# Sampled attention with high and low queries side by side, stacked new values, and GpSimd at work: one change to a decoder-step kernel

## The chip, the cores and the metric

The kernel runs on one core of one Trainium2 chip. The metric is the device time of one execution in microseconds (us). TensorE (PE in the profile) multiplies matrices, VectorE (DVE) and ScalarE (ACT) do elementwise work, GpSimd (POOL) is a further engine that here may touch SBUF only, and SyncE (SP) issues DMAs.

## The reference

One layer of a hybrid decoder, for a prompt of 1024 tokens and for 8 sampled sequences of 8 new tokens each. The change lies in the attention of the sampled sequences, whose 1024 past keys and values lie in 8 pages of 128 rows:

```python
def sample_attn(q, k, v, lam, k_past, v_past, rel_bias):
    ...
    s_past = diff_logits(q, q_pos, k_past, jnp.arange(past, dtype=jnp.int32), rel_bias)
    s_new = diff_logits(q, q_pos, k, q_pos, rel_bias)
    w = diff_weights(jnp.concatenate([s_past, s_new], axis=-1), lam).astype(v.dtype)
    return (jnp.einsum('bhqk,bkhe->bqhe', w[..., :past], v_past)
            + jnp.einsum('bhqk,bkhe->bqhe', w[..., past:], v))
```

`diff_logits` is scaled q.k plus a bias by distance, masked; `diff_weights` is softmax of map 0 minus `lam` times softmax of map 1. There are 8 heads, each with 2 maps of 64 dimensions, so a sequence has 8 heads x 2 maps x 8 tokens = 128 rows of scores over 1032 keys. After it come a norm per head, gates, the output projection, and a channel mixer.

## The kernel before

Every fp32 product is made of reduced-precision (fp32r) ones: an operand is split by ScalarE into a rounded high part (`*_hi`, an `ACT.Copy`) and by VectorE into the rest (`*_lo`, a subtraction), and TensorE adds up hi.hi + hi.lo + lo.hi. The program has four stages: `front` and `heads` (the prompt, up to about 840 us), `sampled_and_out` (the sampled sequences, to about 1105 us, and the output projection), and `mixer`. The change is in `sampled_and_out`.

**Turns and slots.** `all_turns` calls each engine's `body(b, u)` for turns b = 0 to 8. In turn b the scores of sequence b are made (`has(b, 0)`), and the values of sequence b - 1 are multiplied (`has(b, 1)`). A turn runs over slots h: 0 to 8 on TensorE, 0 to 7 on the others. Each engine's queue is in program order, and they meet through counting semaphores. TensorE's slot h does, in order:

- `turn_keys(b, u, h)`: 8 transposes of the raw key pages of head h into two PSUM banks `tb[0]`, `tb[1]`, four each. Each half waits until `kt_lo` of the same half of the head before is made (`ktlo_done`), as it overwrites what that was read from. In slot 8 it is head 0 of the next sequence.
- in slot 0, `page(b - 1, 7)`: the last page of values of the sequence before.
- scores of head h - 1 into the three banks `S3` (344 keys each), which sum over all eight heads: the queries of a head stand in 16 columns of its own of a 128-column block that is otherwise zero, so that each head adds to its own 16 rows. Head 0 waits for `ttr_done`, since VectorE has to have read S3 of the sequence before.
- slot 2: `fold_heads`, 8 products that bring together the two halves of the rows of `o2s` (ScalarE's copy of the attention output `o2`).
- slot 3: `pt`, the weights transposed and signed by a product of P with C; its results are split into `pt_both` in slot 4.
- slots 4 and on: `page(b, n)` for the n of `PV_AT[h]`, 4 products of 512 columns each, which wait until `v_lo` of that page is made. The 8 new rows are a ninth page of 8 rows.

ScalarE's slot h: `keys(b, h)` (two copies to `kt_hi`, each after its half of the transposes, and a small one for the new keys), then in slot 1 the exponent and `copy_o2`, and then the high parts `v_hi` of the pages in `SPLIT_AT[h]`. VectorE's slot h: `keys` (two subtractions to `kt_lo`, and a small one), then `v_lo` of the same pages. At the end of a turn VectorE adds the bias to S3 with a running maximum (`tensor_tensor_reduce`, L2011), negates the maximum, and writes low queries. In turn 7 (`LAST`) both split parts of the output projection too, in the slots of `OUT_AT`, ahead of the pages of the same slot: `("m", 0)` is the first tile of merged activations, loaded by `load_m(0)`. In turn 8 the pages follow `SPLIT_LAST`.

SyncE issues all loads in program order too. In its turn b come the key pages of sequence b + 1 (after `tk_done`, at 16 b), in turns 7 and 8 instead four row blocks of w_out each (`ow_raw`), and in turn 7 then `load_m(0)` and `load_m(1)`; then value page 7 of sequence b - 1, and value pages 0 to 6 of sequence b, each after `page_done` of the same page of the sequence before, since `v_lo`, and with it `v_raw`, is read until then. `load_v(6, ...)` of the turn before, whose last wait is for page 6, stands ahead of `ow_raw` and `load_m(0)`.

GpSimd fills two query tiles with zeros at the stage's start and does nothing else in it.

## Time and profile before

| | us |
|---|---|
| median of 3 runs (lowest, highest) | 2076.24 (2076.22, 2077.07) |
| the profiled execution, its own time | 2075.18 |
| its span in the profile | 2073.4 |
| TensorE busy in the span | 2028.7 (98%) |
| VectorE, ScalarE, GpSimd busy | 1386.3 (67%), 993.4 (48%), 12.4 (1%) |

The spans below are of the one profiled execution, and count from the start of its span. The execution's own time is 1.8 us longer than its span. Busy shares are means over the whole program; what sets the time of a stage is to be read within it. A matmul's listed duration runs over into the next one's; what it costs in a row of matmuls is the distance between two starts.

### The profile page before, as it was taken

How to read it: one execution, taken by the hardware profiler on the slowest of the kernel's cores; microseconds unless marked ns; L12 is line 12 of the kernel's file. 1: busy time of each engine (PE TensorE's matmuls, PEld its weight loads, DVE VectorE, ACT ScalarE, POOL GpSimd, SP SyncE). 2: the span in 40 equal slices, each digit the busy share in tenths (PEclk: the TensorE clock that was granted, in tenths of full speed). 3: DMA queues.
4: the chain of work that ended last, by engine and by line, in shares of the span. 5: the costliest groups of instructions: out<-in, count | busy, mean ns of one | idle time of the engine just before them, and what ended most of it. 6: DMA issues, size and time to landing. Idle time of an engine off the chain costs nothing. (4 is left out here: it accounts for less than half of the span.)

```text
span 2073.4 us, 36494 instructions
## 1 busy us (share of the span) xinstructions
PE 2028.7 (98%) x12160; PEld 1890.0 (91%) x12160; DVE 1386.3 (67%) x3015; ACT 993.4 (48%) x1832; POOL 12.4 (1%) x42
## 2 busy tenths in 40 slices
PE   7999999999999999899999999999999999999998
PEld 6999999999999999899988889999989898989896
DVE  6767676767676767678785467574847484847476
ACT  5757575756575747567775233131314131413133
POOL 0000000000000000000000000000000000000000
PEclk9999999999999999999999999999999999999999
DMA  6411111211111112887772222120202020202012
GB/s 199 139 56 53 56 52 55 62 49 58 49 58 53 56 51 84 309 277 261 277 267 94 72 71 62 32 62 27 65 21 71 21 71 21 61 21 71 12 52 98
DMA packets 167397, 182.82 MB, mean 88 GB/s; under 512 B 11077, under 2 KB 139621, under 8 KB 167317
## 3 DMA queue, kind: packets, MB, share of 16 engines
q1 hardware_dynamic: 166105, 180.98, 27.0%
q8 instruction: 45, 0.74, 0.1%
q10 hardware_dynamic: 1212, 0.81, 0.1%
q14 instruction: 35, 0.29, 0.0%
HBM read 162.56 MB, written 24.46 MB: 90 GB/s over the span
## 5 line engine op out<-in xcount | busy, mean ns | idle before, releaser
L1247 PE MATMUL ps<-h_hi,w_hi 128*128 128x384 f32 (+1 forms) x1152 | 386.8, 336 | 10.2 <-DVE v_lo L1170 6.8
L1247 PE MATMUL ps<-h_hi,w_lo 128*128 128x384 f32 (+1 forms) x1152 | 376.9, 327 | 0.0
L1247 PE MATMUL ps<-h_lo,w_hi 128*128 128x384 f32 (+1 forms) x1152 | 376.7, 327 | 0.0
L2335 PE MATMUL ps<-h_hi,f_w_hi 128*128 128x320 f32 (+1 forms) x1136 | 370.7, 326 | 0.8 <-PEq L1531 0.8
L2335 PE MATMUL ps<-h_hi,f_w_lo 128*128 128x320 f32 (+1 forms) x1136 | 370.4, 326 | 0.0
L2335 PE MATMUL ps<-h_lo,f_w_hi 128*128 128x320 f32 (+1 forms) x1136 | 370.2, 326 | 0.0
L2414 ACT ACTIVATE yc<-ps,f_prm 128x384 f32<-128x384 f32 x144 | 94.0, 653 | 555.9 <-PE ps L2335 401.5
L2315 PE MATMUL ps<-d_hi,act 128*128 128x512 f32 x816 | 257.1, 390 | 1.6 <-DVE d_lo L2518 1.6
L1247 PEld LDWEIGHTS ps<-h_hi,w_hi 128*128 128x128 f32 x1152 | 217.7, 189 | 13.4 <-DVE v_lo L1170 7.2
L1247 PEld LDWEIGHTS ps<-h_lo,w_hi 128*128 128x128 f32 x1152 | 217.3, 189 | 0.6
L1247 PEld LDWEIGHTS ps<-h_hi,w_lo 128*128 128x128 f32 x1152 | 217.0, 188 | 0.0
L2335 PEld LDWEIGHTS ps<-h_hi,f_w_hi 128*128 128x128 f32 x1136 | 213.2, 188 | 1.5 <-issue 1.1
L2335 PEld LDWEIGHTS ps<-h_lo,f_w_hi 128*128 128x128 f32 x1136 | 213.2, 188 | 0.3
L2335 PEld LDWEIGHTS ps<-h_hi,f_w_lo 128*128 128x128 f32 x1136 | 213.2, 188 | 0.0
L2469 DVE TENSOR_TENSOR x<-x,ps 128x512 f32<-128x512 f32 x144 | 98.2, 686 | 151.3 <-PE ps L2315 148.2
L2315 PEld LDWEIGHTS ps<-d_hi,act 128*128 128x128 f32 x816 | 153.2, 188 | 34.0 <-DVE d_lo L2518 1.8
L2315 PE MATMUL ps<-d_lo,act 128*128 128x512 f32 x432 | 168.2, 389 | 0.0
L2540 DVE SCALAR_TENSOR_TENSOR yc<-ps,f_prm,yc 128x383 f32<-128x383 f32 x144 | 82.3, 571 | 94.0 <-ACT yc L2414 90.4
L921 ACT ACTIVATE E<-E,nmx 128x256 f32<-128x256 f32 (+7 forms) x128 | 98.2, 770 | 14.0 <-DVE nmx L1192 10.1
L1188 DVE CUSTOM_DVE_ANT_0 E<-ps,bias 128x256 f32<-128x256 f32 (+7 forms) x128 | 91.4, 751 | 18.6 <-PE ps L1332 18.0
L1958 DVE TENSOR_TENSOR kt_lo<-ps,kt_hi 128x512 fp32r<-128x512 f32 x128 | 82.4, 684 | 31.5 <-ACT kt_hi L1788 31.2
L2315 PEld LDWEIGHTS ps<-d_lo,act 128*128 128x128 f32 x432 | 81.1, 188 | 16.6
(309 smaller groups left out, 3600.3 us busy)
## 6 DMA issues: line engine op xcount, KB each, us to landing
k<-in_cache_k SPq DMA_DIRECT2D x64, 512.0 KB, 5.7
v_raw<-in_cache_v SPq DMA_DIRECT2D x64, 512.0 KB, 4.5
w_raw<-in_w_in SPq DMA_DIRECT2D x48, 512.0 KB, 4.1
f_raw<-in_w_up SPq DMA_DIRECT2D x48, 512.0 KB, 4.0
f_raw<-in_w_down SPq DMA_DIRECT2D x24, 512.0 KB, 3.5
bias<-bias_tiles_dram SPq DMA_DIRECT2D x8, 576.0 KB, 3.8
merged_dram<-mg SPq DMA_DIRECT2D x8, 544.0 KB, 2.7
ow_raw<-in_w_out SPq DMA_DIRECT2D x8, 512.0 KB, 6.4
```

The source lines that it names most:

```text
L921: act.activation(E[i][:, 0:n], E[i][:, 0:n], ACT.Exp, bias=nmx[:, i:i + 1], accum_out=den[:, i:i + 1]).then_inc(exp_done, 1)
L1188: dve.tensor_tensor_reduce(out=halves(E[i], j), in0=scores(i, j), in1=halves(bias, j, c0), scale=1.0, scalar=-3e38, op0=ALU.add, op1=ALU.m ...
L1247: last_ = pe.matmul(bank(s)[:, 0:n], w[:, W_SLOT[g], k, :], x[:, k, off:off + n], start=(k == 0 and i == 0), stop=(k == KT - 1 and i == 2))
L1958: dve.tensor_tensor(kt_lo[:, h % 2, at], tb[hf], kt_hi[:, h % 2, at].bitcast(F32), ALU.subtract).then_inc(ktlo_done, 1)
L2315: l_ = pe.matmul(ps[:, down_bank(e), :], a, w[:, j, 512 * hf:512 * (hf + 1)], start=(j == 0 and i == 0), stop=(j == GF - 1 and i == len(pa ...
L2335: l_ = pe.matmul(ps[:, e % 6, 0:n], w[:, p, k, :], x[:, k, off:off + n], start=(k == 0 and i == 0), stop=(k == KT - 1 and i == 2))
L2414: act.activation(yc[:, e % 3, 0:n], ps[:, e % 6, 0:n], ACT.Identity, bias=prm[:, p, FCONV_W:FCONV_W + 1], scale=prm[:, p, FCONV_W - 1:FCON ...
L2469: dve.tensor_tensor(x2, x2, ps[:, down_bank(e), :], ALU.add).then_inc(add_done, 1)
L2540: link(dve.scalar_tensor_tensor(out=y[:, 1:np_], in0=x[:, 0:np_ - 1], scalar=w[1], in1=y[:, 1:np_], op0=ALU.mult, op1=ALU.add))
```

## The change

- **Scores.** For heads 0 to 3 the columns 0 to 63 of one query tile `qd` hold high queries and the columns 64 to 127 low ones; for heads 4 to 7 it is the other way round. Two products (with `kt_hi`, with `kt_lo`) in place of three then give 64 rows of scores by high queries and 64 by low queries (also low.low, which was not computed before). After four heads ScalarE copies the low rows from PSUM to `slo` (`low_rows`), VectorE adds them to the high rows in S3 and writes P (`sum_rows`), and only then may TensorE start the next four heads in the same banks. At the end of the turn VectorE's `tensor_tensor_reduce` reads P in place of S3.
- **New keys.** They are split once, at the start, into `kn`; GpSimd copies each head's 8 columns into `kt` (`new_key`).
- **New values.** All 64 new rows stand stacked, high in 64 partitions and low in the other 64, in `vn`, loaded and split once; GpSimd lays the new weights of the present sequence in two places of a zeroed tile `p_new` (`new_weights`), and the ninth page takes 2 products of 128 rows in place of 4 of 8 rows.
- **Fold.** `fold_heads` becomes 8 transposes of `o2s` into `o2`'s banks, and VectorE sums the two maps (`fold_rows`, a `reduce_sum` of 128 values per partition); ScalarE's `copy_ot` goes.
- **Pages.** GpSimd makes `v_lo` of pages 2, 5 and 7 in all turns. The slots of `SPLIT_AT` and `PV_AT` change. In ScalarE's slot 1, `copy_o2` comes ahead of the exponent.

```diff
-SPLIT_AT = {2: (0,), 3: (1,), 4: (2, 3), 5: (4, 5), 6: (6,), 7: (7,)}
-PV_AT = {4: (0, 1), 5: (2, 3), 6: (4, 5), 7: (6, NPAGES), 8: ()}
+HH = H // 2
+SPLIT_AT = {2: (0,), 3: (1, 2), 5: (3,), 6: (4, 5), 7: (6, 7)}
+PV_EARLY = {5: (2,)}
+PV_AT = {4: (0, 1), 5: (3,), 6: (4,), 7: (5,), 8: (6, NPAGES)}
+POOL_PAGES = (2, 5, 7)
...
+            def new_key(b, h):
+                if at_start(b) and h == 0:
+                    pool.wait_ge(new_lo, 1)
+                if not (at_start(b) and h < 2):
+                    pool.wait_ge(qkh_done, 8 * b + h - 1)
+                    pool.sem_inc(settled, 1)
+                pool.tensor_copy(kt[:, :, h % 2, PAST:NKEYS], kn[:, :, h, bass.ds(DEC_T * b, DEC_T)])\
+                    .then_inc(ktn_done, 1)
...
+            def body(b, u):
+                for h in range(H):
+                    if has(b, 0):
+                        new_key(b, h)
+                    if h == 2 and has(b, 1):
+                        new_weights(b)
+                    if has(b, 1):
+                        for n in splits_of(b).get(h, ()):
+                            if n in POOL_PAGES:
+                                pool.wait_ge(vhi_done, 8 * (b - 1) + n + 1)
+                                pool.tensor_tensor(v_lo[:, n, :], v_raw[:, n, :], v_hi[:, n, :].bitcast(F32),
+                                                   ALU.subtract).then_inc(vplo_done, 1)
...
                 for g in range(H):
-                    last = pe.matmul(otp[:, DEC_T * g:DEC_T * (g + 1)], o2s[:, 128 * g:128 * (g + 1)],
-                                     fold[:, DEC_T * g:DEC_T * (g + 1)], start=True, stop=True)
+                    last = pe.transpose(o2[:, 128 * g:128 * (g + 1)], o2s[:, 128 * g:128 * (g + 1)], c.ident[:, :])
...
+                    if has(b, 1):
+                        for n in PV_EARLY.get(h, ()):
+                            page(b, n)
                     if h >= 1 and has(b, 0):
                         g = h - 1
                         if g == 0:
                             if not at_start(b):
-                                pe.wait_ge(ttr_done, b)
+                                pe.wait_ge(sum_done, 2 * b)
                             pe.wait_ge(qdlo_done, 4 * b + 2)
-                        if g == H - 2:
+                        if g == HH:
+                            pe.wait_ge(sum_done, 2 * b + 1)
                             pe.wait_ge(qdlo_done, 4 * b + 4)
...
-                            for x, (q, k) in enumerate(((qd_hi, kt_hi), (qd_hi, kt_lo), (qd_lo, kt_hi))):
-                                last = pe.matmul(S3[:, cc, :], q[:, 128 * g:128 * (g + 1)], k[:, g % 2, keys],
-                                                 start=(g == 0 and x == 0), stop=(g == H - 1 and x == 2))
+                            for x, k in enumerate((kt_hi, kt_lo)):
+                                last = pe.matmul(S3[:, cc, :], qd[:, 128 * g:128 * (g + 1)], k[:, g % 2, keys],
+                                                 start=(g % HH == 0 and x == 0), stop=(g % HH == HH - 1 and x == 1))
...
+            def low_rows(b, s):
+                hi, lo = half_rows(s)
+                act.wait_ge(qkh_done, 8 * b + HH * (s + 1))
+                act.activation(slo[hi, :].rearrange("p (a n) -> p a n", a=3), S3[lo], ACT.Copy)\
+                   .then_inc(slo_done, 1)
...
+            def sum_rows(b, s):
+                hi, _ = half_rows(s)
+                dve.wait_ge(slo_done, 2 * b + s + 1)
+                dve.tensor_tensor(P[hi, :].rearrange("p (a n) -> p a n", a=3), S3[hi],
+                                  slo[hi, :].rearrange("p (a n) -> p a n", a=3), ALU.add).then_inc(sum_done, 1)
...
+            def fold_rows(b):
+                dve.wait_ge(ot_done, b + 1)
+                dve.reduce_sum(oT[:, :, bass.ds(DEC_T * b, DEC_T)], own_rows, mybir.AxisListType.X) .then_inc(ots_done, 1)
...
                         for n in splits_of(b).get(h, ()):
+                            if n in POOL_PAGES:
+                                continue
                             dve.wait_ge(vhi_done, 8 * (b - 1) + n + 1)
...
                 if has(b, 0):
-                    dve.wait_ge(qkh_done, 8 * b + 8)
...
+                    sum_rows(b, 1)
+                    dve.wait_ge(sum_done, 2 * b + 2)
+                    dve.sem_inc(settled, 1)
+                    dve.tensor_tensor_reduce(out=P[:, :], in0=P[:, :], in1=sbias[:, :], scale=1.0, scalar=-3e38, op0=ALU.add, op1=ALU.max,
                                              accum_out=mx[:, 0:1]).then_inc(ttr_done, 1)
```

`low_rows(b, 0)` and `sum_rows(b, 0)` stand in slot 4 behind `keys(b, 4)`; `low_rows(b, 1)` and `sum_rows(b, 1)` at the end of the turn behind `keys(b + 1, 0)`. On ScalarE and VectorE the pages of `SPLIT_AT[h]` stand behind `keys(b, h)` as before.

## Rows read from the trace of the kernel before

**Rows 1.** Busy time by stretch: start:end, length, each engine's busy time, clock, DMA.

```profile
core 0: us, PE busy (x) PEld busy (x) DVE busy (x) ACT busy (x) POOL busy (x), PEclk, DMA share, GB/s
840.00:864.60 24.60, 21.68 (x140) 21.27 (x141) 14.19 (x38) 12.34 (x33) 2.06 (x2) 0.86 0.91 330
...
893.77:924.96 31.19, 31.17 (x209) 28.36 (x207) 24.81 (x46) 21.79 (x43) 0.00 (x0) 1.00 0.77 269
...
1049.20:1080.90 31.70, 31.59 (x206) 28.57 (x205) 29.08 (x48) 24.80 (x43) 0.00 (x0) 1.00 0.73 243
1080.90:1104.60 23.70, 23.70 (x120) 19.37 (x119) 18.65 (x23) 16.25 (x20) 0.00 (x0) 1.00 0.57 211
```

**Rows 2.** TensorE in order of time, turns 2 and 3: start, duration, line, operation.

```profile
905.63 1.09 PE L1658 MATMUL ps<-ident,k 128*128 128x128 f32 x8
...
909.84 1.03 PE L1658 MATMUL ps<-ident,k 128*128 128x128 f32 x8
910.63 0.40 PE L1685 MATMUL ps<-kt_hi,qd_hi 128*128 128x344 f32 x1
910.87 0.32 PE L1685 MATMUL ps<-kt_lo,qd_hi 128*128 128x344 f32 x1
...
912.13 0.40 PE L1645 MATMUL ps<-sv_hi,pt_both 128*128 128x512 f32 x1
...
914.00 1.04 PE L1658 MATMUL ps<-ident,k 128*128 128x128 f32 x8
...
921.48 0.49 PE L1645 MATMUL ps<-vn_hi,pt_both 8*128 8x512 f32 x1
...
922.61 1.09 PE L1658 MATMUL ps<-ident,k 128*128 128x128 f32 x8
...
924.96 0.39 PE L1645 MATMUL ps<-sv_hi,pt_both 128*128 128x512 f32 x1
...
930.81 1.85 PE L1633 MATMUL ps<-s_fold,o2s 128*128 128x8 f32 x16
932.51 1.07 PE L1658 MATMUL ps<-ident,k 128*128 128x128 f32 x8
```

**Rows 3.** ScalarE in order of time, turns 2 and 3.

```profile
914.72 1.09 ACT L1788 ACTIVATE kt_hi<-ps 128x512 fp32r<-128x512 f32 x2 [1.09 <-PE ps L1658]
915.68 0.21 ACT L1790 ACTIVATE kt_hi<-k_new 128x8 fp32r x1
915.78 1.06 ACT L1846 ACTIVATE sv_hi<-v_raw 128x1024 fp32r<-128x1024 f32 x1
...
925.25 0.46 ACT L1778 ACTIVATE qd_hi<-q_new 64x16 fp32r x2 [0.69 <-PE ps L1685]
...
928.89 1.00 ACT L1798 ACTIVATE o2s<-ps 128x1024 f32<-128x1024 f32 x1
```

**Rows 4.** VectorE in order of time, turns 2 and 3.

```profile
915.35 1.29 DVE L1958 TENSOR_TENSOR kt_lo<-ps,kt_hi 128x512 fp32r<-128x512 f32 x2 [0.27 <-ACT kt_hi L1788]
...
916.88 1.23 DVE L1996 TENSOR_TENSOR sv_lo<-v_raw,sv_hi 128x1024 fp32r<-128x1024 f32 x1 [0.17 <-ACT sv_hi L1846]
...
925.34 1.23 DVE L2011 CUSTOM_DVE_ANT_0 P<-ps,sbias 128x1032 f32<-128x1032 f32 x1
...
927.25 1.29 DVE L1958 TENSOR_TENSOR kt_lo<-ps,kt_hi 128x512 fp32r<-128x512 f32 x2
```

**Rows 5.** The end of turn 7: VectorE's subtraction for page 7, TensorE's weight load behind it.

```profile
1078.62 1.21 DVE L1996 TENSOR_TENSOR sv_lo<-v_raw,sv_hi 128x1024 fp32r<-128x1024 f32 x1
```

```profile
1079.88 0.19 PEld L1645 LDWEIGHTS ps<-sv_hi,pt_both 128*128 128x128 f32 x1 [0.39 <-DVE sv_lo L1996]
```

**Rows 6.** SyncE's issues, and ScalarE's use of the first merged tile, turns 6 and 7.

```profile
1046.68 1.98 SPq L1589 DMA_DIRECT2D ow_raw<-in_w_out  x4
1048.70 3.13 SPq L1561 DMA_DIRECT2D o_raw<-merged_dram  x2
...
DMA to landing us min/median/max: 9.5/9.5/9.5
```

```profile
1058.50 1.06 ACT L1810 ACTIVATE m_hi<-o_raw 128x1024 fp32r<-128x1024 f32 x1
```

**Rows 7.** GpSimd's instructions by line and shape: count, busy us, mean ns.

```profile
L1534 POOL MEMSET qd_hi<- 128x1152 f32 x1 | 1.1, 1062 | 102.9 <-POOLq L592 102.9
...
L161 POOL TENSOR_SCALAR_AFFINE_SELECT ident<-ident 128x128 f32<-128x128 f32 x1 | 0.3, 292 | 0.2 <-POOL ident L159 0.2
L159 POOL MEMSET ident<- 128x128 f32 x1 | 0.2, 204 | 2.0 <-POOLq L2719 2.0
```

More of the change, by code:

```diff
@@ L1448, in sampled_and_out @@
     qkh_done = sem("qkh_done")
+    slo_done = sem("slo_done")
+    sum_done = sem("s_sum_done")
     ttr_done = sem("s_ttr_done")
@@ L1594, in body @@
                     load_v(b - 1, NPAGES - 1)
-                    if not (isinstance(b, int) and b == 1):
-                        sp.wait_ge(vnlo_done, b - 1)
-                    sp.dma_start(vn_raw[:, :], v_new[bass.ds(DEC_T * (b - 1), DEC_T), :]).then_inc(vn_in, 16)
+                if isinstance(b, int) and b == 1:
+                    for x in range(2):
+                        sp.dma_start(vn_raw[NS * x:NS * (x + 1), :], v_new).then_inc(vn_in, 16)
                 if has(b, 0):
@@ L1816, in body @@
                 for h in range(H):
-                    if h == 3 and has(b, 2):
-                        copy_ot(b - 2)
                     if h == 4 and has(b, 1):
@@ L1835, in body @@
                            .then_inc(exp_done, 1)
-                    if h == 1 and has(b, 2):
-                        copy_o2(b - 1)
                     if h == 1 and isinstance(b, int) and b == DEC_B:
@@ L1855, in body @@
                     keys(b + 1, 0)
-                    act.wait_ge(qkh_done, 8 * b + 8)
-                    queries(b + 1, H - 2, H)
+                if has(b, 0):
+                    low_rows(b, 1)
+                if has(b, 0) and has(b, -1):
+                    queries(b + 1, HH)
             all_turns(act, body)
@@ L1959, in keys @@
                                       ALU.subtract).then_inc(ktlo_done, 1)
[L1960 to L1962 removed]
             def body(b, u):
                 for h in range(H):
+                    if h == 3 and has(b, 2):
+                        fold_rows(b - 2)
                     if h == 4 and has(b, 1):
```

194 lines of the change are left out of this document (107 added, 87 removed).

## The prediction

> **What bounds the kernel now.** I read the stretches first. In a middle turn TensorE is busy 31.17 of 31.19 us, VectorE 24.81, ScalarE 21.79 [rows 1]: TensorE sets the length of a turn, and time taken from it counts as long as nobody makes it wait. Then the order of time on each engine, to see how far ahead of TensorE the others run. Slot 5 begins with transposes at 914.00; ScalarE's `kt_hi` starts 0.72 later and its `v_hi`, behind it in the same slot, at 1.78; VectorE's `v_lo` runs to 918.11, 4.1 after the slot began [rows 2, 3, 4]. Now that does no harm: a page is split one slot or more before it is used. GpSimd is free.
>
> **What TensorE saves.** Nine score products take 912.13 - 910.63 = 1.50 us, the first 0.24 and each further one 0.157 [rows 2]; six take 1.03. That is 0.47 for each of 64 heads, 30.1 us. The ninth page falls from 1.13 (921.48 to 922.61) to two products of 0.234 (a page of four now takes 0.935: 912.13 to 914.00 are two pages), so 0.7 in 8 turns, 5.3. The fold falls from 932.51 - 930.81 = 1.70 to 8 transposes, which cost 0.79 to 0.83 as those of the keys do (909.84 to 910.63), 0.87 in 8 turns, 7.0 [rows 2]. The new weights' transpose stays at two passes. Together 42.4 us, and 5.3 to 5.4 per turn: a middle turn would take some 25.6 us if nothing waited (before, 0.3 of it was the wait for the bias step).
>
> **What the others gain and lose.** VectorE per turn loses 8 small subtractions, three pages of 1.23 and the new values' 1.2, and gets two `sum_rows` at 1.22 (64 x 1032 from PSUM; bound by the bias step's 1.23 for as many elements per partition [rows 4]) and a reduction of 128 elements, some 0.3 (below the 0.65 of a `kt_lo` of 512 [rows 4]). It comes to about 21.5, below 25.6. ScalarE gets two `low_rows` of 1.0 (as `copy_o2`, 1.00 [rows 3]) and loses 8 small copies, about the same sum as before. Neither becomes the bound by its sum. What counts is the order of time.
>
> **The waits, one middle turn.** Call the start of a slot's transposes T. Without the small copy, `v_hi` starts at T + 0.72 + 0.97, ends 1.06 later, `v_lo` starts 0.04 behind it and takes 1.23: T + 4.0 [rows 3, 4]. TensorE goes on 0.05 after a subtraction ends (1079.83 to 1079.88 [rows 5]) and loses 0.1 in restarting.
> - Slot 5 now both splits and uses page 3. TensorE gets there after transposes 0.8, page 2 and scores, 1.9: T + 2.7. It waits 1.4.
> - Slot 6 both splits and uses page 4, and has no page ahead of it: T + 1.8 against T + 4.1. It waits 2.3.
> - Slots 4, 7 and 8 use pages of an earlier slot; no wait.
> - Page 5 is GpSimd's. Its price is not in the trace. Fills take 204 ns for 128 elements and 1062 for 1152, 0.84 ns each; the select, with one input, 292 for 128 [rows 7]. So 1024 elements cost at least a fill's 1.0 us and, with the select's whole 292 scaled less a fixed 0.1 and a second input at 0.84 ns, 1.55 + 0.1 + 0.86 = 2.5; doubling all of the select's for two inputs gives 3.2. I take 2.5, as that row is nearest; range 1.0 to 3.2. `v_hi` of page 5 is there at T + 3.7, and page 5 is wanted after page 4 (T + 5.1), transposes and scores, T + 6.9: hidden up to 2.9 us, at 3.2 it costs 0.3 a turn.
> - Slot 4: `low_rows` starts 0.29 after the last score (924.96 to 925.25 [rows 2, 3]), the sum ends at 2.6. The next scores come two pages, transposes and page 2 later, 3.6: hidden.
> - End of turn. Let E be the end of head 7's scores. `low_rows` ends at E + 1.3, `sum_rows` at 2.55, TensorE may write S3 at 2.6 and gets there at 0.93 + 0.47 + 0.93 (pages 6, new, 7) + 0.8 = 3.1: hidden. But VectorE then does the bias step and what follows, 927.25 - 925.34 = 1.9 [rows 4], before `kt_lo` of head 1: it starts at E + 4.5, its halves end at 5.2 and 5.8. The transposes of head 2 overwrite those banks; TensorE would begin them at E + 4.2 and ends them some 1.3 late. Today `kt_lo` starts at E + 2.3 and is in time. This also covers page 7 if GpSimd is slow. The exponent, one copy later than now, ends at 6.4, the weights' product is at 10: hidden.
>
> Waits are 1.4 + 2.3 + 1.3 = 5.0, and a turn takes 25.6 + 5.0 = 30.6, 0.6 less than 31.2. Five such periods: **-3.0**. Each wait is good to 0.3, the sum of a turn to 0.8, five turns to 4.
>
> **The other turns.** Turn 0 has no pages: its heads are bound by transposes, `kt_hi`, `kt_lo` and back (0.7 + 0.6 + 0.7), 2.03 against 0.8 + 1.5 = 2.3 now [rows 2], but head 4 waits 1.8 for the sum with nothing to cover it, and the keys' split and GpSimd's first copy come ahead of the first scores: **+0.3**. Turn 1 has the end-of-turn wait with no pages before it (transposes of head 2 end about 2.3 later than now, less 0.9 of saved scores), one more split of 1.2 for the stacked values, and then gains 0.9 as the others: **+1.1**.
>
> Turn 7 splits the output weights too, and is where I expect the loss. (a) SyncE issues `load_m(0)` behind `ow_raw` and behind `load_v` of page 6, which waits until that page was used. Page 6 moves from slot 7 (ends 3.4 before E: 921.48 is the product behind it, 924.96 is E; E of turn 6 is at 1049.2, where the stretch of rows 1 begins) to behind E, + 1.1. Now: `ow_raw` 1046.68, `o_raw` 1048.70, landing in 9.5 at 1058.2, in use at 1058.5 [rows 6]: no slack. Then: `ow_raw` at E + 1.9, `o_raw` 2.0 later, landing at E + 13.4, where ScalarE wants it at E + 9.8. `v_hi` 1 and 2 and the weights' split stand behind it in ScalarE's queue; `pt_both` is ready at E + 17.9, and TensorE wants it at 13.9. A wait of 4.1 in slot 4. (b) In slots 5 and 6 an output weight's split is ahead of the page's, + 1.1: T + 5.2, and each slot lasts 6.2. (c) In slot 8 page 6 waits 1.4 and page 7 (GpSimd) 0.8. From E: slot 4 ends at 19.9, slots 5 and 6 at 26.1 and 32.3, slot 7 at 35.1, scores 36.1, the pages at 40.7. Now page 7 ends at 1080.9, E + 31.7 [rows 1]: **+9.0**.
>
> Turn 8: TensorE is busy all of 23.70 us [rows 1] with the others ahead; two folds and the ninth page: **-2.4**.
>
> **Sum.** +0.3 + 1.1 - 3.0 + 9.0 - 2.4 = +5.0 on the profiled execution's own 2075.18 gives 2080.2; the median of the runs shown is 1.06 above that execution, so 2081.2. What a measurement here tells from no change is taken as 0.2%, 4.2 us: the line to slower lies at 2080.4. Bounds: middle turns -4 and +4, turn 7 -4 (the load in time after all) and +2, GpSimd at 3.2 us +2: from 2073 to 2089.
>
> **A rule beside it.** GpSimd's 2.5 us come from its select and fills [rows 7]. The Trainium skill (GPSIMD Engine Reference, Elementwise — side-by-side cycle accounting) has 4497 ns for such a two-input operation of 2048 elements, so about 2.25 us here, an estimate; no run here shows it, and it leaves the sum as it is.
>
> **Rivals.**
> 1. *The page waits are mostly hidden* (ScalarE has the split of pages 3 and 4 done before TensorE's slot gets there). For: ScalarE is free for about 1 us ahead of slot 5's keys. Against: its queue is in order, and `keys` waits for that slot's transposes. Half of 3.7 us in six turns and some of turn 7's waits go: 2081 - 11 - 9 = 2061, 15%.
> 2. *TensorE stays the bound throughout*: 2076.2 - 42.4 = 2034. Against: every wait above. 5%.
> 3. *The merged tile lands in time*, (a) goes: 2081 - 4 = 2077, about no change. For: DMA share is 0.73 in that turn [rows 1], so a landing quicker than 9.5 is possible. 12%.
> 4. *GpSimd's subtraction holds up VectorE whatever that reads.* Page 2's would delay `pt_lo` by 1.9 (TensorE waits 1.7), page 7's the sum by 0.6: 2.3 a turn, 2081 + 16 = 2097. It decides where both overlap at all. Nothing in the trace of before has both at work. The Trainium skill (SBUF — State Buffer, Who interferes with whom) lets only VectorE operations with two SBUF inputs contend, which here would be the pages' subtractions alone; they do not overlap with GpSimd's in the order above. 10%.
> 5. *The clock falls.* It was 0.86 in 840 to 864.6, after TensorE had stood idle there [rows 1]. If waits of 2.3 in slot 6 bring it to the lower level (1.2 GHz), 3 us of TensorE's work a turn run at half rate and cost 3 more, in six turns 18: 2099. 5%.
>
> The likeliest case, the sum with its own range 2073 to 2089, has 50%: 33 slower, 15 within, 2 faster; 3% are left for what I don't see, faster. So faster 0.02 + 0.15 + 0.05 + 0.03 = 0.25, same 0.15 + 0.12 = 0.27, slower 0.33 + 0.10 + 0.05 = 0.48. The range takes in cases 1 and 3 and the bounds, and leaves out 2, 5 and most of 4: 2056 to 2091.
>
> **What would show it.** After: a middle turn of 30.6 from E to E, with 6 score products of 0.157; TensorE idle before `sv_hi` products in slots 5 and 6, put down to VectorE's `sv_lo`, 1.4 and 2.3; before the transposes of head 2, put down to `kt_lo`; in turn 7 ScalarE idle for DMA `o_raw`, 3.6. I am wrong if page products in those slots start without a wait, if turn 7 is no longer than now, if GpSimd's subtraction is over 2.9 us, or if the granted clock falls below 1.00 in middle turns.

## The result, and the profile after

The changed kernel takes 2094.39 us (median of 5, 2093.10 to 2095.54), the kernel before 2076.22 on the same chip: a ratio of 1.0091, 95% interval 1.0079 to 1.0103. It is slower by 18.2 us. The forecast was 2081.2, slower but by 5, with a range that ended at 2091. The profiled execution has a span of 2091.3 against 2073.4, 17.9 longer.

The changed kernel's page, busy times first: TensorE lost 27.4 us of listed work (2028.7 to 2001.3), and the span still grew. So the loss is idle time or work at a lower clock.

```profile
span 2091.3 us, 36003 instructions
...
PE 2001.3 (96%) x11888; PEld 1854.3 (89%) x11888; DVE 1375.2 (66%) x2944; ACT 995.3 (48%) x1770; POOL 93.5 (4%) x146
```

Busy times by stretch of the changed kernel, columns as in [rows 1]: turn 1, turn 2, turn 7 from the end of its predecessor's scores to the last page product, and turn 8. Turn 1 of the kernel before, which [rows 1] leaves out, follows in a fence of its own.

```profile
core 0: us, PE busy (x) PEld busy (x) DVE busy (x) ACT busy (x) POOL busy (x), PEclk, DMA share, GB/s
865.00:903.20 38.20, 26.61 (x149) 23.69 (x150) 22.26 (x35) 21.32 (x35) 7.73 (x10) 0.82 0.71 244
903.20:933.90 30.70, 26.79 (x174) 23.31 (x173) 22.01 (x37) 21.70 (x36) 10.08 (x14) 1.00 0.78 275
1057.13:1099.05 41.92, 31.70 (x176) 26.52 (x175) 28.87 (x39) 26.13 (x38) 13.00 (x15) 0.92 0.56 191
1099.05:1123.20 24.15, 22.23 (x109) 18.24 (x108) 21.24 (x20) 15.18 (x18) 9.24 (x5) 1.00 0.60 232
```

```profile
864.60:893.80 29.20, 28.64 (x189) 25.92 (x188) 24.68 (x46) 20.71 (x41) 0.00 (x0) 1.00 0.90 332
```

Turn 2 has the forecast's shape: 30.70 long with some 4 us of TensorE idle, where before it had none in 31.19 [rows 1]. Turn 7's 41.92 stands against 31.4 before: head 7's scores ended there at 1049.54, 0.34 after the start of the stretch in [rows 1], and the last page product at 1080.92. Turn 8's 24.15 stands against 23.65. Turn 1 is the surprise: 38.2 against 29.2, with a mean clock of 0.82.

A milestone that every kernel has makes a full account. It is the first instruction behind head 7's scores, 0.1 to 0.4 us after their end: ScalarE's second `slo` copy of the turn, or, in kernels with the scores of before, VectorE's bias step. E0 is that of turn 0. Times in us, from one profiled execution each; E1 to E7 are the same point in turns 1 to 7, and "rest" runs from E7 to the end of the span.

| kernel | E0 | E0 to E1 | E1 to E6, per turn | E6 to E7 | rest | span |
|---|---|---|---|---|---|---|
| before | 865.0 | 29.1 | 31.15 | 31.0 | 992.5 | 2073.4 |
| after | 864.4 | 39.2 | 30.75 | 38.8 | 995.1 | 2091.3 |

Turn 0 gives 0.6, turn 1 costs 10.1, the five middle turns give 2.0, and E6 to the end costs 10.5 (turn 7, turn 8 and the rest); together 17.9.

**Turn 1.** First TensorE's transposes of head 2. Then, in order of time, SyncE's issue, and ScalarE, VectorE and TensorE of the changed kernel; the bracket is the engine's idle time before, and what ended it.

```profile
869.41 1.97 PE L1725 MATMUL ps<-ident,k 128*128 128x128 f32 x8 [1.44 <-DVE kt L2036]
...
872.08 1.18 SPq L1661 DMA_DIRECT2D vn_raw<-out_v_rows_sample  x2
...
886.31 1.06 ACT L1920 ACTIVATE vn<-vn_raw 128x1024 fp32r<-128x1024 f32 x1 [6.28 <-DMA vn_raw<-out_v_rows_sample]
887.39 1.08 ACT L1867 ACTIVATE kt<-ps 128x512 fp32r<-128x512 f32 x2
888.36 1.06 ACT L1917 ACTIVATE sv_hi<-v_raw 128x1024 fp32r<-128x1024 f32 x1
...
889.86 1.22 DVE L2083 TENSOR_TENSOR sv_lo<-v_raw,sv_hi 128x1024 fp32r<-128x1024 f32 x1
...
891.13 0.80 PE L1712 MATMUL ps<-sv_hi,pt_both 128*128 128x512 f32 x1 [7.80 <-DVE sv_lo L2083]
...
893.00 1.91 PE L1725 MATMUL ps<-ident,k 128*128 128x128 f32 x8
894.56 2.07 PE L1756 MATMUL ps<-kt,qd 128*128 128x344 f32 x6
```

The DMA list of this stretch (KB each, median us from issue to landing; the two landed after 11.0 and 13.6) and the clock, as in [rows 1]:

```profile
vn_raw<-out_v_rows_sample SPq DMA_DIRECT2D x2, 256.0 KB, 12.3
```

```profile
870.00:872.00 2.00, 2.00 (x10) 2.00 (x9) 1.13 (x4) 1.18 (x3) 0.00 (x0) 0.50 1.05 418
...
888.00:892.00 4.00, 0.87 (x2) 0.78 (x3) 3.04 (x4) 1.42 (x2) 0.00 (x0) 0.50 0.05 20
892.00:896.00 4.00, 4.00 (x16) 3.61 (x16) 1.12 (x2) 1.65 (x3) 0.00 (x0) 0.50 0.37 116
```

Read it backwards. TensorE waits 7.80 us, by the trace for `sv_lo` of page 3. But VectorE only ran that late because ScalarE's `sv_hi` was late, and that stood in ScalarE's queue behind the split of the new values, which waited 6.28 us for their load. The releaser named by the waiting engine is the last link, not the cause. The load is now all 64 rows twice, where it was 8 rows. Its place in SyncE's queue is the same (issued at 871.37 before, at 872.08 now), but it is wanted in slot 4 of turn 1, 8.0 us after its issue (880.03), where it was wanted in slot 6, 14.1 us after (885.47). Then TensorE comes back at a granted clock of 0.50: it had been idle for 7.8 us, and eight transposes take 1.91 and six score products 2.07, against 1.03 and 1.19 in other turns. The clock was also at 0.50 once before the load was wanted, in 870 to 872, and the transposes of head 2 took 1.97 there.

**A middle turn, and turns 7 and 8.** TensorE of the changed kernel: the waits and the fold of turn 3, then the waits of turns 7 and 8.

```profile
939.44 1.25 PE L1725 MATMUL ps<-ident,k 128*128 128x128 f32 x8 [0.57 <-DVE kt L2036]
...
941.48 1.03 PE L1697 MATMUL ps<-ident,o2s 128*128 128x128 f32 x8
942.35 0.82 PE L1725 MATMUL ps<-ident,k 128*128 128x128 f32 x6
...
954.11 0.51 PE L1712 MATMUL ps<-sv_hi,pt_both 128*128 128x512 f32 x1 [1.20 <-DVE sv_lo L2083]
...
959.21 0.50 PE L1712 MATMUL ps<-sv_hi,pt_both 128*128 128x512 f32 x1 [2.07 <-DVE sv_lo L2083]
...
966.56 0.50 PE L1712 MATMUL ps<-sv_hi,pt_both 128*128 128x512 f32 x1 [0.20 <-POOL sv_lo L1599]
...
1073.52 0.50 PE L1712 MATMUL ps<-sv_hi,pt_both 128*128 128x512 f32 x1 [2.44 <-DVE pt_both L2047]
1082.18 0.50 PE L1712 MATMUL ps<-sv_hi,pt_both 128*128 128x512 f32 x1 [2.19 <-DVE sv_lo L2083]
1088.33 0.79 PE L1712 MATMUL ps<-sv_hi,pt_both 128*128 128x512 f32 x1 [3.13 <-DVE sv_lo L2083]
1095.77 0.50 PE L1712 MATMUL ps<-sv_hi,pt_both 128*128 128x512 f32 x1 [1.25 <-DVE sv_lo L2083]
...
1115.17 0.50 PE L1712 MATMUL ps<-sv_hi,pt_both 128*128 128x512 f32 x1 [1.12 <-DVE pt_both L2047]
```

The first rows answer to [rows 2], where none of these waits stood. The fold now takes 0.87 from start to start, not 1.70. In turn 7 ScalarE's copy of the first merged tile, which was in time before [rows 6], waits 2.07:

```profile
1069.07 1.06 ACT L1880 ACTIVATE m_hi<-o_raw 128x1024 fp32r<-128x1024 f32 x1 [2.07 <-DMA o_raw<-merged_dram]
```

### The profile page after: what moved, and what is told of

It reads as the page before. It is cut to its first block and busy times, and to the rows that moved or that the text cites. A ratio compares the mean times of both kernels' runs of the same rounds, so it can differ in the third digit from the quotient of the medians.

```text
span 2091.3 us, 36003 instructions
## 1 busy us (share of the span) xinstructions
PE 2001.3 (96%) x11888; PEld 1854.3 (89%) x11888; DVE 1375.2 (66%) x2944; ACT 995.3 (48%) x1770; POOL 93.5 (4%) x146
## 3 DMA queue, kind: packets, MB, share of 16 engines
q1 hardware_dynamic: 166137, 181.24, 26.7%
## 5 line engine op out<-in xcount | busy, mean ns | idle before, releaser
L1247 PE MATMUL ps<-h_hi,w_hi 128*128 128x384 f32 (+1 forms) x1152 | 386.6, 336 | 10.2 <-DVE v_lo L1170 6.8
L2036 DVE TENSOR_TENSOR kt<-ps,kt 128x512 fp32r<-128x512 f32 x128 | 82.6, 685 | 51.9 <-ACT kt L1867 51.6
L1867 ACT ACTIVATE kt<-ps 128x512 fp32r<-128x512 f32 x128 | 70.4, 598 | 72.9 <-PE ps L1725 69.8
L921 ACT ACTIVATE E<-E,nmx 128x256 f32<-128x256 f32 (+7 forms) x128 | 98.2, 770 | 14.1 <-DVE nmx L1192 10.2
```

The costliest lines, as they stand in the source:

```text
L921: act.activation(E[i][:, 0:n], E[i][:, 0:n], ACT.Exp, bias=nmx[:, i:i + 1], accum_out=den[:, i:i + 1]).then_inc(exp_done, 1)
L1247: last_ = pe.matmul(bank(s)[:, 0:n], w[:, W_SLOT[g], k, :], x[:, k, off:off + n], start=(k == 0 and i == 0), stop=(k == KT - 1 and i == 2))
L1867: act.activation(kt_hi[:, h % 2, 512 * hf:512 * (hf + 1)], tb[hf], ACT.Copy)\
L2036: dve.tensor_tensor(kt_lo[:, h % 2, at], tb[hf], kt_hi[:, h % 2, at].bitcast(F32), ALU.subtract).then_inc(ktlo_done, 1)
```

## The experiments

All are timed beside the kernel before, whose median was 2075.13 beside e1 to e4, 2075.29 beside e5 to e8, 2076.18 beside e9 and e10, 2076.07 beside e11 and e12, and 2076.22 beside the changed kernel. So a difference of two medians from different groups is good to about 1 us, and where it matters the stretches decide. The stretches, as in the table above:

| kernel | median (lowest, highest) | ratio to before, 95% | E0 | E0 to E1 | E1 to E6, per turn | E6 to E7 | rest |
|---|---|---|---|---|---|---|---|
| e1 | 2086.78 (2085.36, 2089.45) | 1.0060 [1.0043, 1.0077] | 865.6 | 30.2 | 30.74 | 39.0 | 995.1 |
| e2 | 2065.37 (2065.18, 2066.82) | 0.9955 [0.9938, 0.9971] | 863.8 | 36.2 | 27.55 | 30.5 | 995.2 |
| e3 | 2091.43 (2088.08, 2095.25) | 1.0079 [1.0062, 1.0096] | 866.0 | 39.3 | 30.74 | 35.4 | 995.1 |
| e4 | 2057.85 (2055.75, 2059.41) | 0.9919 [0.9902, 0.9935] | 864.9 | 28.2 | 27.56 | 28.0 | 995.1 |
| e5 | 2056.38 (2054.70, 2058.17) | 0.9909 [0.9892, 0.9925] | 866.0 | 27.7 | 27.27 | 29.0 | 995.6 |
| e6 | 2054.87 (2053.56, 2057.36) | 0.9905 [0.9889, 0.9922] | 865.3 | 28.2 | 27.55 | 28.0 | 992.6 |
| e7 | 2102.01 (2100.63, 2103.38) | 1.0126 [1.0109, 1.0143] | 865.4 | 30.7 | 33.88 | 42.4 | 993.7 |
| e8 | 2074.22 (2073.46, 2074.99) | 0.9995 [0.9985, 1.0004] | 867.1 | 30.3 | 30.08 | 29.6 | 994.7 |
| e9 | 2085.57 (2084.30, 2087.68) | 1.0045 [1.0028, 1.0062] | 865.3 | 35.9 | 31.12 | 34.2 | 994.9 |
| e10 | 2084.02 (2081.15, 2084.29) | 1.0035 [1.0021, 1.0049] | 868.5 | 31.2 | 31.41 | 31.5 | 994.1 |
| e11 | 2063.93 (2062.82, 2065.54) | 0.9942 [0.9925, 0.9958] | 866.9 | 29.2 | 29.24 | 28.9 | 992.4 |
| e12 | 2054.17 (2053.41, 2055.90) | 0.9899 [0.9883, 0.9916] | 866.6 | 27.7 | 27.27 | 29.0 | 991.9 |

E0 lies between 863.8 and 868.5. Part of that is scatter: the kernels that are the same up to there (after, e2, e3, e9) have 863.8 to 866.0. Part is an effect of e1's edit. At the end of turn 0 TensorE waits for a load of keys in e1, e4, e5, e6, e10, e11 and e12 (1.60, 1.42, 1.03, 1.08, 2.95, 1.80 and 1.79 us), which all load the new values early, ahead of five pages of keys on SyncE, and in none of before, after, e2, e3, e7 and e9. Only e8, whose turn 0 has more products, loads early without that wait. The early load is not free, and stretches are compared here, not spans.

**e1: the new values loaded early.**

```diff
                 sp.dma_start(mg[:, :, :], ...).then_inc(const_in, 16)
+                for x in range(2):
+                    sp.dma_start(vn_raw[NS * x:NS * (x + 1), :], v_new).then_inc(vn_in, 16)
...
-                if isinstance(b, int) and b == 1:
-                    for x in range(2):
-                        sp.dma_start(vn_raw[NS * x:NS * (x + 1), :], v_new).then_inc(vn_in, 16)
```

> The changed kernel, with the two loads of the new values (vn_raw) moved from turn 1 of the attention, where they stand in SyncE's queue behind the key and value pages, to the loads of the constants ahead of turn 0. Theory A (the late load made turn 1 long: ScalarE's split of the new values waited 6.3 us for it, TensorE then 7.8 us for value page 3, and its clock fell): both waits go, the stretch from the end of turn 0's scores to the end of turn 1's falls from 39.1 to about 30.5 us, and the kernel takes about 2086 us (8 to 9 less than 2094.4). Theory B (turn 1 is long because the first page waits and GpSimd's first subtractions fall there, and the load only shows up as the last releaser): page 3 is still waited for by over 4 us, and the time stays within 2 us of 2094.4.

E0 to E1 is 30.2 in place of 39.2, and the median falls by 7.6. TensorE's waits for the transposes of head 2 and for page 3 in turn 1 of e1:

```profile
870.63 1.25 PE L1724 MATMUL ps<-ident,k 128*128 128x128 f32 x8 [1.45 <-DVE kt L2035]
...
884.97 0.50 PE L1711 MATMUL ps<-sv_hi,pt_both 128*128 128x512 f32 x1 [1.58 <-DVE sv_lo L2082]
```

Theory A holds: 1.58 is near the 1.20 of a middle turn. The 9.0 us can be divided by the two traces. 6.2 are the shorter wait for page 3 (7.80 to 1.58), less 0.8 for a longer one for page 4 (1.17 to 2.00). 2.5 are the work between the two waits, which takes 5.5 in the changed kernel, where the clock was 0.50, and 3.0 in e1. The other 1.1 us is the low clock in 870 to 872: from the first scores of turn 1 to its first page product it is 11.67 in the changed kernel and 10.54 in e1, behind nearly the same waits. It lies ahead of the point where the load is wanted. It comes again in e2 and e3 and not in e9, which all have the late load too, and in none of the kernels that load early; whether e1's edit took it away is not shown. So some 8 of the 9 us are the late load. Whether its size or its earlier slot made it late was not tried apart; landing when it did (886.3), it would have been 0.8 late even for the slot of before.

**e2: each page split a slot ahead.**

```diff
-SPLIT_AT = {2: (0,), 3: (1, 2), 5: (3,), 6: (4, 5), 7: (6, 7)}
+SPLIT_AT = {2: (0,), 3: (1, 2), 4: (3,), 5: (4, 5), 6: (6,), 7: (7,)}
```

> The changed kernel with its table of splits alone altered: value page 3 is split in slot 4 instead of slot 5, pages 4 and 5 in slot 5 instead of 6, page 6 in slot 6 instead of 7, so that each page is split one slot ahead of its product. Theory A (the saving of TensorE in the middle turns, 4.0 us by its removed products, is eaten by the waits for pages 3 and 4 that the table places, 1.2 and 2.1 us a turn, and by products that wait behind them): the period falls from 30.7 to 27.0 to 27.5 us in five middle turns, turn 7 loses 5 or more of its waits, and the kernel takes about 2070 us (2064 to 2076), faster than before. Theory B (the period is set by the chain key copies, splits and weights on ScalarE and VectorE, whatever their order): the waits come back at the key tiles or the transposes, the period stays above 30 us, and the time within 5 us of 2094.4.

One line of a table gives 29.0 us (27.9 if each median is first set against its own kernel before) and makes the change a gain. The middle turns fall from 30.75 to 27.55, E6 to E7 from 38.8 to 30.5, turn 1 from 39.2 to 36.2 (its load is still late). TensorE in a middle turn of e2:

```profile
899.90:927.27 27.37, 26.12 (x173) 23.46 (x173) 21.94 (x37) 21.90 (x36) 10.90 (x15) 1.00 0.85 309
```

The others do the same work as in the changed kernel (VectorE 21.94 against 22.01, ScalarE 21.90 against 21.70), only in another order, and the turn is 3.2 shorter. Theory B falls.

**e3: the output stage's first loads early.**

```diff
                 if has(b, -1):
+                if isinstance(b, int) and b == LAST - 1:
+                    for t in range(2):
+                        load_m(t)
...
-                if isinstance(b, int) and b == LAST:
-                    for t in range(2):
-                        load_m(t)
```

> The changed kernel with the two first loads of the merged heads for the output stage (load_m) issued at the start of turn 6's issues on SyncE instead of in turn 7 behind the wait for the weights' buffer. Theory A: ScalarE's wait of 2.1 us for this load in turn 7 goes, and with it part of TensorE's waits of 2.4 and 2.2 us there: 2 to 4 us less, 2090 to 2092. Theory B (turn 7 is held by the number of splits on ScalarE and VectorE, not by the load): the wait of the load goes and TensorE's waits for value pages grow by as much, the time stays within 1 us of 2094.4.

E6 to E7 falls by 3.4, the median by 3.0. The single times of e3 spread over 7 us and reach those of the changed kernel (2093.1 to 2095.5), so it is the stretch that carries this. ScalarE no longer waits for the tile, and TensorE's wait for the weights, 2.44 in the changed kernel, is 0.32; its waits for pages (2.20, 3.13, 1.24) are what they were. Theory A holds.

**e4: the three together.**

> The changed kernel with the three edits of the other runs together: new values loaded ahead of turn 0, the table of splits one slot earlier, the first loads of the output stage in turn 6. Theory A (placement ate the saving of TensorE): the gains add, about 2058 us (2052 to 2066), some 18 faster than before, and TensorE is busy all through the middle turns. Theory B (the work of ScalarE, VectorE and GpSimd in a turn is the bound once TensorE's work is shorter): the time is above 2070 us, with waits for other tiles in the places of those taken away.

2057.85, in the expected range and 36.5 below the changed kernel; the single edits give 7.6, 29.0 and 3.0, together 39.6. By the stretches 1.0 us of their gains is shared in turn 1 (9.0 and 3.0 alone, 11.0 together) and 1.0 in turn 7 (8.3 and 3.4, 10.8 together). TensorE is not busy all through a turn: it still waits at the turn's end, 0.9 to 1.4 us before the transposes of head 2, and for GpSimd's small copy of keys:

```profile
953.40 1.25 PE L1724 MATMUL ps<-ident,k 128*128 128x128 f32 x8 [1.38 <-DVE kt L2035]
...
971.75 1.22 PE L1755 MATMUL ps<-kt,qd 128*128 128x344 f32 x6 [0.35 <-POOL kt L1576]
```

**e5: VectorE makes all pages again** (e4 with this edit).

```diff
-POOL_PAGES = (2, 5, 7)
+POOL_PAGES = ()
```

> The kernel of e4 with GpSimd's share of the value pages (2, 5 and 7) given back to VectorE, so that VectorE subtracts all eight. VectorE's busy time in a middle turn of e4 is 22.2 us of 27.5; three more subtractions of 1.21 us make 25.8, TensorE's is 26.1. Theory A (with the splits a slot ahead, GpSimd's share is not what carries the gain): period 27.5 to 28.5 us, turn 8 about 1 us shorter because VectorE's subtractions there no longer take 2.7 to 3.2 us, in all 2056 to 2066. Theory B (VectorE is the next bound and its share must go elsewhere): period above 29 us, and the kernel above 2068.

No clear difference from e4 (2056.38). VectorE is busy 25.33 of 27.45 us in a middle turn, GpSimd 2.86, and the turn is 0.3 shorter: the waits for GpSimd's copy of keys are gone, and shorter ones for the low part of the weights (0.24 to 0.47) have come. Turn 7 is 1.0 longer. Theory A holds for the middle turns: GpSimd's share of the pages carries none of the gain. Its forecast for turn 8, 1 us shorter, failed, as the rest is 0.5 longer, although VectorE begins the low part of the weights at E7 + 14.4, where it was E7 + 18.2 in e4. What holds turn 8 is now the sum of the fold (`s_oT`), behind three pages in VectorE's queue. TensorE waits 1.90 for it and goes on at a clock of 0.51; first e4, then e5:

```profile
1070.79 0.43 PE L1768 MATMUL ps<-C,p_new 128*128 128x64 f32 x2 [1.59 <-DVE s_oT L2018]
```

```profile
1071.31 0.69 PE L1768 MATMUL ps<-C,p_new 128*128 128x64 f32 x2 [1.90 <-DVE s_oT L2018]
```

**e6: turn 8 without GpSimd's pages, its fold a slot earlier** (on e4).

```diff
-                        for n in splits_of(b).get(h, ()):            # GpSimd
+                        for n in () if isinstance(b, int) and b == DEC_B else splits_of(b).get(h, ()):
...
-                            if n in POOL_PAGES:                      # VectorE
+                            if n in POOL_PAGES and not (isinstance(b, int) and b == DEC_B):
                                 continue
...
-                    if h == 3 and has(b, 2):
+                    if h == (2 if isinstance(b, int) and b == DEC_B else 3) and has(b, 2):
                         fold_rows(b - 2)
```

> The kernel of e4 with, in turn 8 alone, all eight pages subtracted by VectorE (GpSimd has none there), and with the fold of the finished heads' rows put one slot earlier on VectorE in that turn. Theory A (VectorE and GpSimd reading two operands each from SBUF hinder one another: in e4 VectorE's two pages beside GpSimd take 6.40 us, against 1.2 us for one alone, and the low part of the weights comes late by it): every page takes 1.2 us on VectorE, the low part of the weights is ready 2 to 3 us earlier, TensorE starts on the pages 1.5 to 2.7 us earlier, and the stretch from the end of head 7's scores to the end of the kernel shrinks from 995.1 by as much; the kernel takes about 2055.5. Theory B (the two are slow for another reason, such as where they read, or TensorE's products of the output stage set this stretch anyway): less than 0.5 us of it.

The rest falls from 995.1 to 992.6, as theory A forecast, but this run has two edits, and the cause is not that theory's alone. Pages in turn 8, first in e4, with VectorE and GpSimd side by side, then in e6, on VectorE alone:

```profile
1070.70 6.40 DVE L2082 TENSOR_TENSOR sv_lo<-v_raw,sv_hi 128x1024 fp32r<-128x1024 f32 x2
...
1073.23 6.12 POOL L1599 TENSOR_TENSOR sv_lo<-v_raw,sv_hi 128x1024 fp32r<-128x1024 f32 x2 [0.57 <-ACT sv_hi L1916]
```

```profile
1069.84 4.62 DVE L2082 TENSOR_TENSOR sv_lo<-v_raw,sv_hi 128x1024 fp32r<-128x1024 f32 x4
1074.38 0.69 DVE L2044 TENSOR_TENSOR pt_both<-ps,pt_both 128x512 fp32r<-128x512 f32 x1
```

VectorE takes 6.40 us for two pages beside GpSimd, and in e6 4.62 for four. The low part of the weights stands behind them: at 1074.38 in e6, at 1077.02 in e4. So the two engines do hinder each other. The gain is another matter: GpSimd's pages taken out without the earlier fold (e5) gave nothing, and the earlier fold with all pages on VectorE (e12 against e5, which differ in nothing else) takes 3.7 us from the rest. In e4 TensorE waits 1.59 for the fold's sum and 1.14 for the weights; in e6 0.46 and nothing. It takes both edits; the earlier fold beside GpSimd's pages was not run.

**e7: the change's tables alone, in the kernel before.**

```diff
-SPLIT_AT = {2: (0,), 3: (1,), 4: (2, 3), 5: (4, 5), 6: (6,), 7: (7,)}
-PV_AT = {4: (0, 1), 5: (2, 3), 6: (4, 5), 7: (6, NPAGES), 8: ()}
+SPLIT_AT = {2: (0,), 3: (1, 2), 5: (3,), 6: (4, 5), 7: (6, 7)}
+PV_AT = {4: (0, 1), 5: (2, 3), 6: (4,), 7: (5,), 8: (6, NPAGES)}
```

> The kernel before with nothing but the change's tables of slots (pages 1 and 2 split in slot 3, page 3 in slot 5, pages 4 and 5 in slot 6, pages 6 and 7 in slot 7; page 6 and the new values multiplied in slot 8, page 5 in slot 7, page 4 in slot 6). Theory A (the tables cost waits for pages 3 and 4 whatever TensorE has to do): 3 to 4 us per turn are added, since TensorE has no slack there, and the time is 2095 to 2104. Theory B (the waits appear only because the change makes TensorE's slots shorter): 2075 to 2081.

Page 2's product stays behind the scores of slot 5 here, as in the kernel before. 26.7 us more than before with the arithmetic untouched, so theory A holds: 2.7 per middle turn (less than the 3 to 4 expected) and 11.4 in turn 7. TensorE in two turns of e7, where `sv_lo` is waited for in a middle turn and `pt_both` in turn 7:

```profile
984.80 0.50 PE L1645 MATMUL ps<-sv_hi,pt_both 128*128 128x512 f32 x1 [0.76 <-DVE sv_lo L1996]
989.98 0.49 PE L1645 MATMUL ps<-sv_hi,pt_both 128*128 128x512 f32 x1 [1.71 <-DVE sv_lo L1996]
...
1083.66 0.49 PE L1645 MATMUL ps<-sv_hi,pt_both 128*128 128x512 f32 x1 [3.15 <-DVE pt_both L1970]
```

**e8: a third product back** (on e4; the product with the low part of the keys is made twice, so that part counts double in the scores).

```diff
-                            for x, k in enumerate((kt_hi, kt_lo)):
+                            for x, k in enumerate((kt_hi, kt_lo, kt_lo)):
```

> The kernel of e4 with a third product per score block again: each head's scores take the product with the low part of the keys twice (so this part counts double in the scores), which gives TensorE the nine products per head that the kernel before had, and leaves everything else as in e4. Theory A (with the pages in time, TensorE sets the turn, and its removed products are worth their full length): 8 times 0.47 us per turn less the 1.4 us of waits that it may hide, so 2.4 to 3.8 us per turn over eight turns, 2077 to 2088. Theory B (another engine sets the turn of 27.5 us): less than 1.5 us per turn, under 2070.

2.52 us per middle turn and 16.4 in all: the turn as theory A has it, the time of 2074.22 some 3 us under its lower figure of 2077. TensorE is busy 29.52 us of 30.10, where e4 has 26.10 of 27.50: 3.4 more. Its waits shrink by some 0.8 (at the turn's end from about 1.0 to about 0.6, and 0.35 for GpSimd's copy to nothing). So TensorE sets e4's turn, and what is taken from it there is worth three quarters of its listed length.

**e9: the changed kernel with the tables of before.**

> The changed kernel with all three tables of slots put back as they were before (pages 2 and 3 split in slot 4, 4 and 5 in slot 5, 6 in slot 6, 7 in slot 7; products of pages 0 and 1 in slot 4, 2 and 3 in 5, 4 and 5 in 6, 6 and the new values in 7, 7 at the turn's end), so that only the arithmetic of the change is left. Theory A (the arithmetic is worth its TensorE time and the tables cost what they cost in the kernel before, 26.7 us): period 27.3 to 27.8 us, turn 7 30 to 31 us, turn 1 still long (35 to 37 us) for the late load of the new values, in all 2062 to 2070, faster than before by some 10. Theory B (the tables were what made the new arithmetic fit, and the old ones would make other waits): 2080 or more.

2085.57 is theory B's figure: the old tables do make other waits. The period is 31.12, as long as before. I had read the old tables as like those of e2, and they are not: they split pages 2 and 3 both in slot 4, one after the other on ScalarE, and use page 2 in slot 5; with a shorter slot 4 and 2.4 us for GpSimd's subtraction that is too late. In e9's middle turns TensorE waits 1.17 for page 2 and 0.95 for page 3. It follows that the change's own tables are not the only ones that spoil it: with the old ones the changed kernel is 8.8 us faster than with its own, and still 9.4 slower than the kernel before, with the late load still in it (turn 1 takes 35.9).

**e10: e6 with the tables of before.**

> The kernel of e6 with the tables of before, as in e9. Against e6 only TensorE's order of page products differs (pages 2, 5, 6 and the new values a slot earlier) and nothing of VectorE's and ScalarE's splits. Theory A (once each page is split a slot ahead, where TensorE multiplies it does not matter): within 2 us of e6, 2053 to 2057. Theory B (the later products are what keeps TensorE from waiting): 2060 or more, with waits for pages 3, 5 or 6.

The expectation's premise was wrong in the same way: page 2's split moved too. 2084.02 is theory B's figure, but it says nothing on the products. Four of the five middle turns take 30.9 to 31.1 us, one 32.9. These are waits of TensorE in e10, for pages 2 and 3:

```profile
949.56 0.50 PE L1711 MATMUL ps<-sv_hi,pt_both 128*128 128x512 f32 x1 [1.12 <-POOL sv_lo L1599]
954.61 0.50 PE L1711 MATMUL ps<-sv_hi,pt_both 128*128 128x512 f32 x1 [0.95 <-DVE sv_lo L2082]
```

**e11: e6 with the old tables of products, splits as in e6.**

```diff
-PV_EARLY = {5: (2,)}
-PV_AT = {4: (0, 1), 5: (3,), 6: (4,), 7: (5,), 8: (6, NPAGES)}
+PV_EARLY = {}
+PV_AT = {4: (0, 1), 5: (2, 3), 6: (4, 5), 7: (6, NPAGES), 8: ()}
```

> The kernel of e6 with only the two tables of products put back as before (page 2 after the scores of slot 5 instead of ahead of them, page 5 in slot 6, page 6 and the new values in slot 7), and the splits left as in e6. This is what e10 was to be; there page 2's split had moved with it, from slot 3 to slot 4. Theory A (what decides is how far each split stands ahead of its product, and one slot is enough): every page is still a slot ahead, the period stays at 27.5 to 28.2 us, in all 2054 to 2060. Theory B (the later products themselves shorten the turn): above 2065, as e10's 2084.

Between the two theories: 2063.93. In the middle turns only one wait for a page is left, 0.16 at 1036.07, so most of e10's loss was the split of page 2. But 9 us remain, and they sit at the turn's end, in e11:

```profile
927.23 1.22 PE L1755 MATMUL ps<-kt,qd 128*128 128x344 f32 x6 [0.51 <-DVE P L2005]
929.75 1.25 PE L1724 MATMUL ps<-ident,k 128*128 128x128 f32 x8 [1.31 <-DVE kt L2035]
```

With page 6 and the new values behind E, TensorE has 1.4 us more to do while the rows are copied and summed; that order of products does earn something. In two of the five turns the transposes behind this wait also ran slower (1.97 and 1.71 us; the granted clock was 0.52 in 960 to 962), and these two turns take 30.2 and 30.3, the other three 28.5 to 28.6.

**e12: e6 with all pages on VectorE.**

> The kernel of e6 with no page subtracted by GpSimd in any turn. Theory A (GpSimd's share buys nothing once the splits stand a slot ahead): the same as e6 within 1.5 us, 2053 to 2056; the wait of 1.9 us that e5 had in turn 8 for the fold of the rows is gone. Theory B (VectorE's queue is then too long in some turn): 2058 or more.

2054.17, the same as e6, as theory A has it: 1.0% below the kernel before, 1.9% below the changed one.

## Why the prediction was wrong

**The step that failed is turn 1's "+1.1".** It counts for the stacked new values "one more split of 1.2" and nothing else. It measured +10.1. The prediction costed the split and left out the load that feeds it: in the same place on SyncE, grown from one DMA of 8 rows to two of 64, wanted two slots earlier, and issued at 872.08 behind key pages, with the DMA engines at a share of 1.02 (872 to 878). The second of the two landed 13.6 us after its issue, at 886.3; ScalarE wanted it at 880.0. e1 takes this load out of turn 1, and turn 1 comes to 30.2, which is 1.0 above before. Of the 9.0 between them some 8 are the load (6.2 - 0.8 of waits, 2.5 of low clock behind them) and 1.1 a low clock ahead of it that is not explained. The +1.1 itself does not follow from its terms: 2.3 - 0.9 + 1.2 - 0.9 is 1.7, so that it agrees with e1's 1.0 is partly luck. The same rule was applied to `load_m` in turn 7 and not here. With 9 more in this term the sum would have been 2090.

**Rival 5, the clock,** was placed in middle turns and given 5%. There it stayed at 1.00. It fell behind 7.8 us of idleness in turn 1 (0.50), in parts of turn 7 (0.72 to 0.90), and in 870 to 872, behind waits of 1.19 and 1.44. Rival 5 had the right mechanism in the wrong turns.

**Middle turns:** 30.6 forecast, 30.75 measured; -2.0 in place of -3.0. That the turn came so near is in part luck. TensorE was busy 26.8 of it, where 25.6 was forecast, and idle 3.9, where 5.0 was; two misses of over 1 us cancel. The waits stood where they were forecast: page 3 waits 1.20 (1.4 forecast), page 4 2.07 (2.3), the transposes of head 2 0.57 to 0.91 (1.3). A few tenths were not foreseen: 0.20 for GpSimd's page 7. Six score products take 1.03, the fold 0.87, the two `sum_rows` 1.24 each, GpSimd's page 2.47 to 2.50 against the 2.5 chosen. e2 confirms which term ate the saving: when the waits for pages 3 and 4 go, the turn is 27.55, of which 26.1 is TensorE's work. Over the whole program TensorE's listed work is 38.4 us less in e4 than before, against 42.4 forecast.

**Turn 7:** +10.5 against +9.0; with the right start of the turn before (1049.54, not 1049.2) the forecast's own figure would be +9.3. (a) was 2.07 of waiting on ScalarE against 3.6, and 2.44 on TensorE against 4.1; the tile was in use 8.4 us after its issue, where 9.5 had been taken for the landing. e3 prices it at 3.4. (b) slots 5 and 6 waited 2.19 and 3.13. (c) was 1.25 and 0.59 against 1.4 and 0.8. All waits of TensorE come to 10.2 us (41.92 - 31.70), where the forecast has some 14 (40.7 less 26 of work), and TensorE is busy 31.70, a little more than before (31.27), with some 5 us less to do. So the lowered clock, which the forecast left out, fills the place of the shorter waits, and here too the total is nearer than its parts. The larger lesson is e7: in the kernel before, the same tables cost 11.4 there.

**Turn 8:** +0.5 against -2.4. The forecast counts two folds in it, but the second stands behind turn 8's last page product, and its saving of 0.9 belongs there: from that product to the end it is 968.1, 968.8 before. So -1.5 was to be had in turn 8 and -0.7 arrived behind it. The saved products are there, but TensorE waits 0.80 for the fold's sum and 1.12 for the low part of the weights. VectorE and GpSimd worked on pages at the same time, which the prediction said they would not, and the fold's sum stood behind two of VectorE's pages; e6 mends both and gives 2.5 back, and with e12 turn 8 is 21.8, 1.9 below before. Rival 4's mechanism was at work here, in the form of its last sentence: it is VectorE's operations with two inputs from SBUF that slow down (3.2 us a page beside GpSimd, 1.2 alone). `kt<-ps,kt`, with one from PSUM, keeps its 0.64 a half at 961.76 in e4, where GpSimd's page runs from 960.08 to 962.57. The Trainium skill (SBUF — State Buffer, Who interferes with whom) has it so, and these two readings agree with it. The same section also names VectorE's two-port modes, which the prediction's "only" leaves out; no run here shows them. That the pages' subtractions are the only such operations here was a misreading of the kernel: the splits of the output weights have two inputs from SBUF too, and the one at 1096.19 in turn 7, beside GpSimd's page 7, took 2.85. What was also wrong was to apply the order of a middle turn to turn 8, where `SPLIT_LAST` splits pages 1 to 4 within two slots.

**Turn 0:** -0.6 against +0.3, which is within the scatter of E0.

**Rival 1** (page waits hidden, 2061) did not happen, but e2 shows that it was one line away. **Rival 2** (TensorE the bound, 2034) did not come true even with every page in time: e12's 2054 is 20 us above it, for the end-of-turn waits and turns 1, 7 and 8.

By parts: the arithmetic of the change is worth some 20 us once its inputs are there (e6 and e12 against before). Its own tables take all of it back, measured against e2's (29.0), and against the old ones in the kernel before (26.7, e7); in the changed kernel the old ones are only 8.8 better than its own (e9). The late load takes 7.6 and the late tile 3.0. It was not one thing that does not pay, but a good thing placed a slot too late.

## What to carry to other kernels

When products are taken from the engine that sets the time, its slots get shorter, and every operand that was made one slot ahead with a little to spare is now late; move the makers ahead by as much, and look at the table of due slots before the arithmetic. Price each part with its load: where a split moves or grows, follow its DMA back through the queue that issues it. And before giving work to an idle engine, see whether the busy one had slack anyway (VectorE did: with all pages it is busy 25.3 of 27.5) and whether the two read the same memory at once.
